# Turning tiles in the RWKV recurrence: 64x64 products with a two-block identity in place of 128x128 and 128x64 turns

## The reference, cut to what matters

```python
def rwkv7_scan(r, w, k, v, kk, a, S):
    def step(S, inp):
        rt, wt, kt, vt, kkt, at = inp
        sa = jnp.einsum("bhvk,bhk->bhv", S, -kkt)
        S = S * wt[:, :, None, :] + sa[..., None] * (kkt * at)[:, :, None, :] + vt[..., None] * kt[:, :, None, :]
        return S, jnp.einsum("bhvk,bhk->bhv", S, rt)
    S, ys = lax.scan(step, S, xs)
```

## Time and profile before

| what | value |
|---|---|
| median of the timed runs | 3282.19 us (3281.83 to 3284.26) |
| span of the profiled execution | 3285.7 us |
| instructions in it | 64217 |
| TensorE matmul busy | 3046.9 us (93%) x25576 |
| TensorE weight load busy | 2487.9 us (76%) x25576 |
| VectorE / ScalarE / GpSimd busy | 72% / 54% / 18% |
| granted clock of TensorE, mean | 0.956 |
| the recurrence's stage | 1062 to 1374 us: 312 us |

### The profile page before, as it was taken

The page is one execution under the profiler, slowest core; times in us unless marked ns, Lnnn a source line. Parts: engine busy times, 40 slices in busy tenths (PEclk is TensorE's granted clock), DMA queues, the critical chain, the costliest instruction groups (busy, mean ns, idle before and its releaser), DMA issues. The chain is left out here.

```text
span 3285.7 us, 64217 instructions
## 1 busy us (share of the span) xinstructions
PE 3046.9 (93%) x25576; PEld 2487.9 (76%) x25576; DVE 2351.2 (72%) x3467; ACT 1767.9 (54%) x2875; POOL 575.5 (18%) x620
## 2 busy tenths in 40 slices
PE   6998889999797998879999999998999999999998
PEld 4774568878673787769977898866788888888887
DVE  5868754468747344577847677654799999999998
ACT  2424343232314554345436444764788888888877
POOL 0007123421100333138213111430000000000000
PEclk8998989999898999989979998998999999999999
DMA  6536224446221000158732788402899999999996
GB/s 220 170 108 20 103 84 154 138 148 208 90 64 26 4 5 4 36 200 275 273 90 78 278 315 300 126 27 79 321 368 368 371 368 367 373 364 374 366 359 263
DMA packets 337363, 647.53 MB, mean 197 GB/s; under 512 B 23853, under 2 KB 144281, under 8 KB 337113
## 3 DMA queue, kind: packets, MB, share of 16 engines
q1 hardware_dynamic: 316233, 568.38, 51.0%
q0 software_dynamic: 20160, 73.41, 6.1%
q10 hardware_dynamic: 720, 2.23, 0.2%
HBM read 641.34 MB, written 1.05 MB: 196 GB/s over the span
## 5 line engine op out<-in xcount | busy, mean ns | idle before, releaser
L5008 DVE TENSOR_TENSOR weights_lo<-raw_ring,weights_hi 128x1024 fp32r<-128x1024 f32 x336 | 401.1, 1222 | 35.5 <-ACT weights_hi L4938 28.3
L4938 ACT ACTIVATE weights_hi<-raw_ring 128x1024 fp32r<-128x1024 f32 x336 | 356.7, 1065 | 90.0 <-PE bank_pair L4874 53.6
L5008 DVE TENSOR_TENSOR weights_lo<-H,weights_hi 128x1024 fp32r<-128x1024 f32 x224 | 268.9, 1223 | 24.6 <-ACT weights_hi L4938 17.4
L4874 PE MATMUL bank_pair<-weights_hi,expert_x_hi 128*128 128x512 f32 x896 | 281.7, 395 | 4.9 <-DVE weights_lo L5008 4.8
L4874 PE MATMUL bank_pair<-weights_hi,expert_x_lo 128*128 128x512 f32 x896 | 277.2, 391 | 0.0
L4874 PE MATMUL bank_pair<-weights_lo,expert_x_hi 128*128 128x512 f32 x896 | 276.8, 390 | 0.0
L4938 ACT ACTIVATE weights_hi<-H 128x1024 fp32r<-128x1024 f32 x224 | 236.5, 1060 | 58.1 <-PE bank_pair L4874 43.2
L2704 DVE SCALAR_TENSOR_TENSOR conv<-bank_pair,vec,conv 128x189 f32<-128x189 f32 (+3 forms) x396 | 138.6, 432 | 144.6 <-ACT conv L2664 144.6
L4874 PEld LDWEIGHTS bank_pair<-weights_lo,expert_x_hi 128*128 128x128 f32 x896 | 168.5, 188 | 36.1
L4874 PEld LDWEIGHTS bank_pair<-weights_hi,expert_x_lo 128*128 128x128 f32 x896 | 168.5, 188 | 35.9
L4874 PEld LDWEIGHTS bank_pair<-weights_hi,expert_x_hi 128*128 128x128 f32 x896 | 163.8, 189 | 36.0 <-issue 5.0
(11 more groups left out here) (803 smaller groups left out, 8160.5 us busy)
## 6 DMA issues: line engine op xcount, KB each, us to landing
raw_ring<-in_moe_w_gate SPq DMA_DIRECT2D x64, 1024.0 KB, 6.5
raw_ring<-in_moe_w_up SPq DMA_DIRECT2D x56, 1024.0 KB, 7.2
ring_up<-in_ffn_w_up SPq DMA_DIRECT2D x110, 512.0 KB, 4.3
H<-in_moe_w_down SPq DMA_DIRECT2D x48, 1024.0 KB, 5.1
raw_ring<-in_moe_w_down SPq DMA_DIRECT2D x48, 1024.0 KB, 5.1
mod_ring_ada<-in_w_ada POOLq DMA_DIRECT2D x84, 512.0 KB, 6.5
ring_down<-in_ffn_w_down SPq DMA_DIRECT2D x66, 512.0 KB, 6.5
H<-in_moe_w_gate SPq DMA_DIRECT2D x32, 1024.0 KB, 7.2
```

The costliest lines, as they stand in the source:

```text
L4874: ins = nc.tensor.matmul(bank, x[:, k * SEATS:(k + 1) * SEATS].bitcast(F32R), w[:, j * WIDE:(j + 1) * WIDE], start=k == 0 and i == 0, stop ...
L4938: nc.scalar.activation(hi[:, u % CUTS].bitcast(F32R), raw_part(u), ACT.Copy).then_inc(cut.sem, 1)
L5008: nc.vector.tensor_tensor(lo[:, u % CUTS].bitcast(F32R), raw_part(u), hi[:, u % CUTS], ALU.subtract).then_inc(parted.sem, 1)
```

## The change: what it does, and the diff

All turns go through `cross`, that is, as eight 64x64 products per unit (four pairs of heads times two halves), with the head's 64x64 block as the stationary operand and `pair_ident` as the moving one. `pair_ident` is a [128, 64] constant: the 64x64 identity twice, one above the other. The values' turn, four 128x64 products before, becomes the same eight products. The results lie in `slot`s, 128 columns in each of the unit's two banks (KAPPA 0, BETA 1, V 2, D 3), in place of `cell`s. Since a quadrant's output half is chosen by s and its bank by r, the heads come out in another order: ScalarE's copies get other access patterns, with the same number of elements, and the readers of `d` take `turned_at(k)` in place of `k`. Waits, steps and their order stay as they are.

```diff
--- before.py
+++ after.py
@@ -3140,9 +3140,9 @@
         last = {(d, g): core.sb(f"last_{d}{g}", [P, 2, N], ctx=ctx)[:] for d, g in RW_UNITS}
         for u, unit in enumerate(RW_UNITS):
             keys, sources = (st.H[:, 2 * u + i].rearrange("p (two n t) -> p two n t", two=2, n=N) for i in (0, 1))
-            turned = core.sb(f"turned_{unit[0]}{unit[1]}", [P, 2, N, C], ctx=ctx)[:]
+            turned = core.sb(f"turned_{unit[0]}{unit[1]}", [P, 2 * N, C], ctx=ctx)[:]
             T[unit].update(keys=keys, alpha=keys[:, 0], rho=keys[:, 1], sources=sources, beta=sources[:, 0], state=sources[:, 1],
-                           turned=turned, kappa_t=turned[:, 0], beta_t=turned[:, 1])
+                           turned=turned, kappa_t=turned[:, 0:N], beta_t=turned[:, N:2 * N])
             T[unit].update(u=T[unit]["c"], w=T[unit]["lk"], grow=wide[unit][:, :, 1:C + 1])
         sync = ScanSteps(core)
         chain, zeroed = core.counter("vector_chain"), core.counter("rw_zeroed")
@@ -3168,9 +3168,19 @@
 
             return psum[unit][rows, :, n * 4 * C:(n + 1) * 4 * C].rearrange("p r (j two t) -> p r j two t", j=2, two=2)
 
-        def cell(unit, r, area, rows=slice(0, P)):
-
-            return psum[unit][rows, r, area * N * C:(area + 1) * N * C].rearrange("p (n t) -> p n t", n=N)
+        def halved_slot(unit, n, level, which):
+
+            flat = psum[unit][:, :, n * 2 * C:(n + 1) * 2 * C]
+            return flat.rearrange("p r (b two h) -> p r b two h", two=2, h=1 << (level - 1))[:, :, :, which]
+
+        def halved(x, level, which):
+
+            flat = x.rearrange("p (r j) t -> p r (j t)", r=2)
+            return flat.rearrange("p r (b two h) -> p r b two h", two=2, h=1 << (level - 1))[:, :, :, which]
+
+        def turned_at(k):
+
+            return k % 2 * 2 + k // 2
 
         def by_slot(x):
 
@@ -3188,10 +3198,9 @@
 
             return slot(unit, n)[:, :, :, 0:C // 2]
 
-        D_AT = {1: (0, 1), 2: (1, 1), 3: (0, 1), 4: (1, 1), 5: (0, 1)}
-        SLOT = {"V": 2, "Y": 1, "E": 0, "U": 0, "R": 2, "O": 3, "S": 1}
+        SLOT = {"KAPPA": 0, "BETA": 1, "V": 2, "Y": 1, "D": 3, "E": 0, "U": 0, "R": 2, "O": 3, "S": 1}
         TABLE, READ, SOURCE = 0, 1, 0
-        CELL_V = (0, 1)
+        SAME = st.C("pair_ident").unsqueeze(1).to_broadcast([P, N, C])
 
         @block.tensor
         def _(pe):
@@ -3218,7 +3227,7 @@
                     for s in (0, 1):
                         for r in (0, 1):
                             k = 2 * j + s
-                            ins = nc.tensor.matmul(packed(out[HALF[s], r, j], level), x[HALF[r], k], y(HALF[r], k), start=True, stop=True)
+                            ins = nc.tensor.matmul(packed(out[HALF[s], r, j], level), x(HALF[r], k), y(HALF[r], k), start=True, stop=True)
                 return ins
 
             def own(out, x, y):
@@ -3228,10 +3237,7 @@
                 return ins
 
             def turn(out, x):
-                for j in (0, 1):
-                    pair = slice(2 * j, 2 * j + 2)
-                    ins = nc.tensor.transpose(out[:, pair].rearrange("p n t -> p (n t)"), x[:, pair].rearrange("p n t -> p (n t)"), st.C("ident"))
-                return ins
+                return cross(out, [(x, SAME)])
 
             for it, step, units in rwkv_order("pe"):
                 latent, fresh = rwkv_kinds(it)
@@ -3254,12 +3260,10 @@
                             ins = cross(wide_slot(unit, TABLE)[:, :, :, 0], [(t["beta"], alpha)])
                     elif step == "KB":
                         sync.wait(pe, "dve", unit, *((it - 1, "S") if it else (it, "CT")))
-                        turn(cell(unit, 0, 0), t["kappa"])
-                        ins = turn(cell(unit, 1, 0), t["beta"])
+                        turn(slot(unit, SLOT["KAPPA"]), t["kappa"])
+                        ins = turn(slot(unit, SLOT["BETA"]), t["beta"])
                         if fresh:
-                            for k in range(N):
-                                to = cell(unit, *CELL_V, HALF[k % 2])[:, k // 2 * 2:k // 2 * 2 + 2]
-                                ins = nc.tensor.matmul(to, rw.v[:, g * N + k, chunk(d, it)[1]], st.C("ident"), start=True, stop=True)
+                            ins = turn(slot(unit, SLOT["V"]), rw.v[:, mine(g), chunk(d, it)[1]])
                     elif step == "LK":
                         sync.wait(pe, "act", unit, it, "V" if fresh else "KB")
                         if latent:
@@ -3280,15 +3284,15 @@
                             sync.wait(pe, "dve", unit, it, "W")
                         else:
                             sync.wait(pe, "dve", unit, it, f"E{l - 1}")
-                        ins = cross_late(slot(unit, SLOT["Y"]), l, t["c"], lambda rows, k: half_columns(t["e"][rows, k], l, 1 - d))
+                        ins = cross_late(slot(unit, SLOT["Y"]), l, lambda rows, k: t["c"][rows, k], lambda rows, k: half_columns(t["e"][rows, k], l, 1 - d))
                     elif kind == "D":
                         l = int(step[1])
                         sync.wait(pe, "act", unit, it, f"Y{l + 1}")
-                        ins = turn(cell(unit, *D_AT[l]), t["e"])
+                        ins = turn(slot(unit, SLOT["D"]), t["e"])
                     elif kind == "E":
                         l = int(step[1])
                         sync.wait(pe, "act", unit, it, f"D{l - 1}")
-                        ins = cross_late(slot(unit, SLOT["E"]), l, t["d"], lambda rows, k: packed(t["y"][rows, k], l))
+                        ins = cross_late(slot(unit, SLOT["E"]), l, lambda rows, k: t["d"][rows, turned_at(k)], lambda rows, k: packed(t["y"][rows, k], l))
                     elif step == "U":
                         sync.wait(pe, "dve", unit, it, f"E{RW_LEVELS[-1]}")
                         ins = own(slot(unit, SLOT["U"]), t["e"], t["w"])
@@ -3334,18 +3338,17 @@
                         elif step == "LKV":
                             ins = nc.scalar.activation(by_slot(t["lk"]), slot(unit, SLOT["V"]), ACT.Copy)
                         elif step == "KB":
-                            ins = nc.scalar.activation(t["turned"], psum[unit][:, :, 0:N * C].rearrange("p r (n t) -> p r n t", n=N), ACT.Copy)
+                            ins = nc.scalar.activation(by_slot(t["turned"]), psum[unit][:, :, 0:N * C].rearrange("p r (x t) -> p r x t", t=C), ACT.Copy)
                         elif step == "V":
-                            ins = nc.scalar.activation(val_t(unit, it), cell(unit, *CELL_V), ACT.Copy)
+                            ins = nc.scalar.activation(by_slot(val_t(unit, it)), slot(unit, SLOT["V"]), ACT.Copy)
                         elif kind == "Y":
                             ins = nc.scalar.activation(by_slot(t["y"])[:, :, :, 0:C // 2], packed_slot(unit, SLOT["Y"]), ACT.Copy)
                         elif kind == "D":
                             l = int(step[1])
                             if l == 1:
-                                ins = nc.scalar.activation(t["d"], cell(unit, *D_AT[l]), ACT.Copy)
+                                ins = nc.scalar.activation(t["d"].rearrange("p (r j) t -> p r j t", r=2), slot(unit, SLOT["D"]), ACT.Copy)
                             else:
-                                flat = lambda x: x.rearrange("p n t -> p (n t)")
-                                ins = nc.scalar.activation(half_columns(flat(t["d"]), l, d), half_columns(flat(cell(unit, *D_AT[l])), l, d), ACT.Copy)
+                                ins = nc.scalar.activation(halved(t["d"], l, d), halved_slot(unit, SLOT["D"], l, d), ACT.Copy)
                         elif step == "U":
                             ins = nc.scalar.activation(by_slot(t["u"]), slot(unit, SLOT["U"]), ACT.Copy)
                     sync.done(ins, "act", unit)
```

## The result

The changed kernel took 3357.34 us (median, 3348.74 to 3359.81), the kernel before beside it 3282.01 us (3279.25 to 3284.26). The ratio is 1.0224, with a 95% interval of 1.0208 to 1.0240: slower by 75 us. The forecast was 3353 us.

The account below looks back on a forecast made before the run. It took TensorE's instruction supply, in blocks of 256, to bind: +73 us for blocks after 1087 us, -2 at the start, all else 0, gave +71 on the median 3282.2, so 3353 us; 80% range 3322 to 3380.

Parts of the forecast that it names:

- The limit: TensorE in the changed stage: supply of instructions in blocks of 256 binds, not the array; 80%, own range 3325 to 3375.
- the array reading: TensorE's array time decides the stage, so its 21 us saving comes out: 3261 us, faster; 8%.
- The count: TensorE records in the stage: 6528 more, 25.5 blocks; 104 or 105 instruction packets expected.
- The price of a block: After 1087 us: 99.0 blocks at 3.64 us make 360 us against 287, +73; ends 3.41 and 3.78 us.
- The first rival: TensorE's blocks come in time, perhaps loaded on demand, so the 21 us of array time come out: 3261 us; 8%.
- What hides the array's gain: TensorE in the stage: 21 us of saved array time worth nothing, as the engine only waits longer at each border.
- The start: Stage until 1087 us: 5 blocks, 18 us, fit under the 25 us there; saved array time counts, -2 us.
- ScalarE's copies and the banks: Some 250 stage copies with longer patterns, output in both banks: hidden, 0; at most +12 us if nothing covered them.
- The clock: TensorE's granted clock in the stage stays up, 0; rival that stalls lower it: 3375, up to 3400 us, 6%.
- Outside the stage: After the stage: the rest starts later but unchanged, 0.

Follow-up runs that it names:

- Experiments 2, 3 and 4: In order: turns_twice; turns_bf16; the kernel before with only D turns (3330.83 us), or only KB and values' turns (3291.50 us), as 64x64 products.
- turns_twice: The changed kernel with every turn's products issued twice, the second writing the same values again: 3464.39 us, ratio 1.0568 to the kernel before.
- v_packed_again: Repeat run: kernel before with values' turn as two 128x128 transposes, GpSimd first copying four value tiles side by side: 3274.40 us, ratio 0.9980.
- d_only: The kernel before with only the D turns (160 of the 240) as 64x64 products, KB and values as before: 3330.83 us, ratio 1.0167.
- turns_bf16: The changed kernel with turns on operands' upper 16 bits as bfloat16, one load and one matmul record per product: 3305.77 us, ratio 1.0092.

## Why the prediction was right

**The limit.** The prediction split "TensorE is busy" into array and supply, and let supply decide. That step carried the result: the array reading gives 3261 us and the wrong sign. Experiments 2, 3 and 4 show it, each away from the array reading, and the gaps at borders of 256 show where the time goes.

**The count.** 6528 records more: the trace has exactly 3264 + 3264. 104 packets against "104 or 105".

**The price of a block.** Taken 3.64 us from the densest window; measured 3.69 us between fetches from 1087 us on. On 98 to 99 blocks that is 5 us too little, about as much as the 4 us between 3353 and 3357. The 3.78 us of the mean would have given 3367, the 3.41 us of the fastest stretch 3331; that the error is only 4 us owes something to luck. The first rival supposed that loads are started on demand. They do follow the crossing of a border, by 1.14 us, but the block is then not usable for another 2.4 us, so the price did not fall.

**What hides the array's gain.** 21 us of array time were counted as nothing. The gaps at borders grew by 86 us (18 to 104) while the stage grew by 76 us (end of the stage at 1451.5 in place of 1375.0): what the array and the other engines' waits gave back went into the gaps. That is some 10 us for both together, under the 21 us estimated for the array alone; no run measures these 21 us by themselves.

**The start.** Costed at -2 us. In the first 25 us 1492 records passed, where 824 + 456 = 1280 would have been the same place in the program. But the stage began 1.2 us earlier in this execution, at 1063.67 in place of 1064.87. From its first product to that same place it took 22.3 us before and 20.3 after: -2 us, as costed. The reason is open: the granted clock of these 25 us was 0.89 in place of 0.73, and the lower level ended 3.9 us into the stage in place of 10.9, so saved array time is not the only candidate.

**ScalarE's copies and the banks.** 0, and the means moved by 2 ns or less.

**The clock.** Costed at 0 with 6% for the case that it falls. It did fall a little, 1.00 to 0.96 after 1087 us, in five stretches of 3 to 10 us. Eight intervals between packets lie mostly in these; they average 3.87 us, against 3.67 for those wholly at 2.4 GHz, which makes some 2 us in all. So the term was close to nothing, but the grant did not hold.

**Outside the stage.** The span grew by 70.4 us and the stage by 76.5. The rest after the stage took 1904.6 us in the profile after and 1910.7 in that before, while it took 1899.7 us in turns_twice and 1899.4 in v_packed_again: the untouched rest differs by several us between executions, so single spans are no measure of a few us here.

The Trainium skill's rule (Runtime: NRT & Kernel Launch, Instruction fetch mechanics) that crossing a 16 KiB border is mostly hidden does not hold in this stage, by the 94 stalled borders. That of draining at a change of tiling mode (TensorEngine Tiling (Array Packing), Tiling Modes) agrees with the 0.15 and 0.20 us before the change; no run here shows a gain from leaving these out.

## What to carry to other kernels

Count instructions per engine as well as their time. Where an unrolled stage like this one asks TensorE for more than 256 records (loads and matmuls both count) in about 3.7 us, a form with more instructions loses, even if the estimate makes it the faster one on the array. The sign to look for is gaps put down to "issue" that cut a step in two, a whole multiple of 256 records apart, with packets of the instruction queue evenly spaced. Small float32 products cost four records each (two loads, two matmuls), a transpose two.

## What the runs showed of the hardware that was not expected

- Where blocks are awaited, the mean period between instruction packets is nearly the same in every kernel: 3.69 (changed kernel), 3.71 (turns_twice), 3.73 (d_only) and 3.74 us (turns_bf16), single ones from 3.25 to 4.8 us. In the changed kernel a packet starts 1.14 us after the engine resumes at a border, and the engine resumes 2.42 us after a packet's start (medians).
- The granted clock of the stage was 0.98 before, 0.95 in the changed kernel, 0.88 with 16-bit turns, 0.59 and 0.50 with all products on 16 bits, although TensorE was busy 241 of 290 us in the first of these two by the modelled ends. Stalls alone don't account for it: turns_twice, with 30 more packets to wait for than the changed kernel, was granted 0.96. What does is open.
- `nop` with fusion off added no instruction packets to the stage (80 against 79), while a one-column stand-alone weight load takes 10 ns (0.14 us for 14).
